# Per-head decays from running sums, with three small steps moved from VectorE to ScalarE, in a two-layer mLSTM/SSD trunk

## The reference

```python
acs = jnp.cumsum((dt * a_neg).reshape(bsz, nc, L, ng, ne), axis=2)
ah = jnp.transpose(acs, (0, 1, 3, 4, 2))
decay = jnp.exp(jnp.where(causal, ah[..., :, None] - ah[..., None, :], -jnp.inf))
y_intra = jnp.einsum('bcgts,bcgets,bcsgep->bctgep', cb, decay.astype(x.dtype), xw)
y_inter = (jnp.einsum('bctgn,bcgepn->bctgep', cc, s_start.astype(x.dtype))
           * jnp.exp(acs)[..., None].astype(x.dtype))
...
w_intra = jnp.exp(dlog - m_t[..., None])          # mLSTM: weights of the scores
ha = rmsnorm(ha, g_mlstm_head[i]).reshape(bsz, s_len, M_INNER) * jax.nn.sigmoid(o_pre)
```

## Time and profile before

| | |
|---|---|
| median of 3 runs | 1561.26 us (1561.2 to 1562.8) |
| profiled execution: its own time, its span | 1561.38 us, 1559.6 us |
| PE busy, share of the span | 1538.0 us, 99% |
| PEld busy | 1439.7 us, 92% |
| DVE busy | 1073.6 us, 69% |
| ACT busy | 809.2 us, 52% |
| POOL busy | 153.5 us, 10% |
| granted TensorE clock, mean | 0.999 of full |
| DMA | 271.09 MB, 174 GB/s mean |
| the mixing block's groups, layer 0 | 208 us to 453 us after the start |

### The profile page before, as it was taken

The page is one execution under the profiler, slowest core; times in us unless marked ns, Lnnn a source line. Parts: engine busy times, 40 slices in busy tenths (PEclk is TensorE's granted clock), DMA queues, the critical chain, the costliest instruction groups (busy, mean ns, idle before and its releaser), DMA issues.

```text
span 1559.6 us, 28133 instructions
## 1 busy us (share of the span) xinstructions
PE 1538.0 (99%) x11594; PEld 1439.7 (92%) x11594; DVE 1073.6 (69%) x1314; ACT 809.2 (52%) x1141; POOL 153.5 (10%) x147
## 2 busy tenths in 40 slices
PE   7999999999999999999999999999999999999998
PEld 6999999999999979999899999998999999799996
DVE  5556578889887546565765556799888866555556
ACT  6444385664655355443564445755766633544444
POOL 1000011233130000000000000113243100000001
PEclk9999999999999999999999999999999999999999
DMA  8665554456455556655565555454544465466551
GB/s 253 195 198 192 175 158 110 146 153 186 135 157 190 193 168 204 200 188 190 166 192 192 194 196 165 123 156 136 188 134 152 153 206 197 149 211 195 199 189 69
DMA packets 245089, 271.09 MB, mean 174 GB/s; under 512 B 12560, under 2 KB 226152, under 8 KB 245012
## 3 DMA queue, kind: packets, MB, share of 16 engines
q1 hardware_dynamic: 239504, 266.90, 53.6%
q10 hardware_dynamic: 5364, 2.98, 0.7%
q0 software_dynamic: 144, 0.15, 0.0%
HBM read 268.94 MB, written 1.05 MB: 173 GB/s over the span
## 4 chain that ended last, share of the span: by engine, by line
PE 90%; DVE 4%; issue 3%; ACT 2%; DMA 1%; SPq 0%; POOL 0%; ACTq 0%; POOLq 0%; DVEq 0%
PE bank L1562 29%; PE bank L1646 28%; PE bank L1592 8%; PE bank L1593 8%; PE bank L1594 8%; PE bank L1995 1%; PE bank L1587 1%; PE bank L1850 1%; DVE w_lo L936 1%; PE bank L1578 1%; PE bank L1580 1%; PE bank L1579 1%; ACT w_hi L530 1%; DVE xcv L1174 1%; DMA w_raw<-in_w_ffn_dram 1%
## 5 line engine op out<-in xcount | busy, mean ns | idle before, releaser
L936 DVE TENSOR_TENSOR w_lo<-w_raw,w_hi 128x2048 fp32r<-128x2048 f32 x248 | 576.9, 2328 | 315.8 <-ACT w_hi L530 315.5
L530 ACT ACTIVATE w_hi<-w_raw 128x2048 fp32r<-128x2048 f32 x248 | 474.1, 1916 | 307.4 <-PE bank L1646 131.0
L1646 PE MATMUL bank<-f_lo,w_hi 128*128 128x256 f32 x1280 | 355.6, 278 | 0.0
L1646 PE MATMUL bank<-f_hi,w_lo 128*128 128x256 f32 x1280 | 353.5, 276 | 0.0
L1646 PE MATMUL bank<-f_hi,w_hi 128*128 128x256 f32 x1240 | 342.6, 276 | 0.0
L1562 PE MATMUL bank<-u_hi,w_hi 128*128 128x256 f32 x1152 | 326.6, 283 | 1.3 <-DVE w_lo L936 1.3
L1562 PE MATMUL bank<-u_lo,w_hi 128*128 128x256 f32 x1152 | 319.9, 278 | 0.0
L1562 PE MATMUL bank<-u_hi,w_lo 128*128 128x256 f32 x1152 | 319.9, 278 | 0.0
L1646 PEld LDWEIGHTS bank<-f_hi,w_lo 128*128 128x128 f32 x1280 | 240.4, 188 | 0.0
L1646 PEld LDWEIGHTS bank<-f_lo,w_hi 128*128 128x128 f32 x1280 | 240.4, 188 | 0.0
L1646 PEld LDWEIGHTS bank<-f_hi,w_hi 128*128 128x128 f32 x1240 | 232.8, 188 | 0.0
(11 more groups left out here) (308 smaller groups left out, 2453.8 us busy)
## 6 DMA issues: line engine op xcount, KB each, us to landing
w_raw<-in_w_ffn_dram SPq DMA_DIRECT2D x262, 512.0 KB, 4.3
w_raw<-in_w_in_dram SPq DMA_DIRECT2D x160, 512.0 KB, 4.9
w_raw<-in_w_branch_b_dram SPq DMA_DIRECT2D x32, 512.0 KB, 4.4
w_raw<-in_w_branch_a_dram SPq DMA_DIRECT2D x16, 512.0 KB, 4.5
w_raw<-in_w_out_dram SPq DMA_DIRECT2D x16, 512.0 KB, 4.1
w_raw<-in_w_ple_gate_dram SPq DMA_DIRECT2D x16, 512.0 KB, 4.3
y_feat<-in_w_ple_dram ACTq DMA_DIRECT2D x2, 1024.0 KB, 4.9
h<-in_x_dram SPq DMA_DIRECT2D x2, 512.0 KB, 5.5
```

Of the source, the lines that this page charges most:

```text
L530: a_.activation(whi[slot][:, :, :], raw[slot][:, :, :], ACT.Copy).then_inc(sem["w_hi"], 1)
L936: v_.tensor_tensor(wlo[slot][:, :, :], raw[slot][:, :, :], whi[slot][:, :, :].bitcast(F32), ALU.subtract).then_inc(sem["w_lo"], 1)
L1646: i = mm(o, four(w[slot])[:, k, cs], x[:, rows0 + k, :], start=opens, stop=(not start and k == 3 and q == 2), skip_group_check=True)
```

## The change

Decays: a new matmul group in `gates(lay)`, once a layer, makes the running sums of all 32 heads as rows of `acs` (16 matmuls of 128 columns from `twin`, high and low part, with 40 stationary columns); ACT copies them out (`sums_high`), DVE subtracts the low part (`sums_low`). In each group PE then spreads a head's row over the partitions with `pick` (`sums(half)`: four matmuls of 256 columns, both chunks at once). ACT makes the distance by a Relu with the token's own sum as its bias (`acol`), one instruction for each head and chunk, then the exponentials. `R_hi`, `R_lo`, `segments` and `from_start` go. The scores' distances, the scaling of the normed heads and the output gate's last step go from DVE to ACT. DVE's order changes.

```diff
-                    def segments(c, half):
-
-                        pe.wait_ge(sem["r_built"], G * 4 + (2 * c + half + 1))
-                        mm(bank[4 + 2 * c + half][:, :], tri_gt_r[:, :], R_hi[half][:, :, :], start=True, stop=False)
-                        mm(bank[4 + 2 * c + half][:, :], tri_gt_r[:, :], R_lo[half][:, :, :], start=False, stop=True)\
-                            .then_inc(sem["seg_done"], 1)
-
-                    def from_start():
-                        for half in range(2):
-                            pe.wait_ge(sem["exp_done"], G * 4 + (3 + half))
-                            mm(bank[6 + half][:, :], ones_r[:, :], R_hi[half][:, :, :], start=True, stop=False)
-                            mm(bank[6 + half][:, :], ones_r[:, :], R_lo[half][:, :, :], start=False, stop=True)\
-                                .then_inc(sem["seg_done"], 1)
+                    def sums(half):
+
+                        if first:
+                            pe.wait_ge(sem["acs_ready"], lay + 1)
+                            pe.wait_ge(sem["pick_ready"], lay + 1)
+                            pe.wait_ge(sem["cum_exp"], lay + 1)
+                        elif half == 0:
+                            pe.wait_ge(sem["st_ready"], G)
+                            pe.wait_ge(sem["num1_ready"], G)
+                        else:
+                            pe.wait_ge(sem["y_ready"], G)
+                        for e in range(4):
+                            i = mm(bank[4 + 2 * half + e // 2][:, (e % 2) * S:(e % 2 + 1) * S], pick[half][:, e, :],
+                                   acs[:, bass.ds(g, 1), :].rearrange("p a b -> p (a b)"), start=True, stop=True)
+                        i.then_inc(sem["seg_done"], 1)
...
+                pe.wait_ge(sem["dA_split"], lay + 1)
+                for g in range(NG):
+                    for c in range(NC):
+                        o = bank[4 + g // 2][0:40, (g % 2) * S + c * P:(g % 2) * S + (c + 1) * P]
+                        mm(o, twin[0][:, c, g, :], tri_le_r[:, :], start=True, stop=False)
+                        i = mm(o, twin[1][:, c, g, :], tri_le_r[:, :], start=False, stop=True)
+                i.then_inc(sem["acs_done"], 1)
...
+                    def decay(half):
+
+                        act.wait_ge(sem["seg_done"], G * 2 + (half + 1))
+                        for e in range(4 * half, 4 * half + 4):
+                            for c in range(NC):
+                                i = a_.activation(seg[:, c, e, :], bank[4 + e // 2][:, (e % 2) * S + c * P:(e % 2) * S + (c + 1) * P],
+                                                  ACT.Relu, scale=-1.0, bias=acol[:, c, bass.ds(g * EH + e, 1)])
+                        i.then_inc(sem["gap_ready"], 1)
+                        for e in range(4 * half, 4 * half + 4, 2):
+                            a_.activation(cs[:, e:e + 2, :], two(4 + e // 2)[:, :, P:2 * P], ACT.Exp)
+                        act.wait_ge(sem["gap_ready"], G * 2 + (half + 1))
+                        a_.activation(seg[:, :, 4 * half:4 * half + 4, :], seg[:, :, 4 * half:4 * half + 4, :],
+                                      ACT.Exp, scale=-1.0).then_inc(sem["exp_done"], 1)
 
                     def score_exp():
+                        act.wait_ge(sem["gtk_ready"], G + 1)
+                        act.wait_ge(sem["scores_done"], G + 1)
+                        for c in range(NC):
+                            i = a_.activation(pm[:, c, :], bank[3][:, S + c * P:S + (c + 1) * P], ACT.Relu, bias=gtk[:, c:c + 1])
+                        i.then_inc(sem["d_ready"], 1)
                         act.wait_ge(sem["d_ready"], G + 1)
                         a_.activation(pm[:, :, :], pm[:, :, :], ACT.Exp, scale=-1.0).then_inc(sem["p_exp"], 1)
...
+                    def heads_normed():
+                        act.wait_ge(sem["hsc_ready"], G + 1)
+                        for c in range(NC):
+                            i = a_.activation(num[:, c, 0:MV], num[:, c, 0:MV], ACT.Copy, scale=hsc[:, c:c + 1])
+                        i.then_inc(sem["hn_ready"], 1)
...
+                    act.wait_ge(sem["group_ready"], G + 1)
+                    act.wait_ge(sem["o_tanh"], G * 3 + 1)
+                    for t in range(2):
+                        a_.activation(osg[:, t, :], osg[:, t, :], ACT.Identity, scale=ghn[:, t:t + 1], bias=ghn[:, t:t + 1])\
+                            .then_inc(sem["o_tanh"], 1)
...
                     else:
                         dve.wait_ge(sem["taps_ready"], G + 1)
                         evac(BC, xin[:, 0, :, 3:])
+                        step(1)
+                        queries_and_keys()
                         taken(BC)
                         conv(0, 0, (0, 1), bcv[:, :, :])
-                        queries_and_keys()
-                        step(1)
+                        step(2)
                         silu(0, bcv[:, :, :])
-                        step(2)
-                        distances()
                         step(3)
...
                         conv(2, 0, (4, 5), xcv[:, 2:4, :])
+                        mask_cb()
                         silu(2, xcv[:, 2:4, :])
-                        mask_cb()
                         step(4)
                         dve.wait_ge(sem["ysum_ready"], G + 1)
                         evac(Z0, zs[:, 0:2, :])
+                        weighted_inputs()
                         step(5)
-                        weighted_inputs()
                         gate_half(0)
```

More of the change, by code:

```diff
@@ L112, in trunk @@
         top[0] = place(feat_at, 512, 1024)
+        ha_hi_at = top[0]
         ha_hi = sb("ha_hi", [P, 2 * MH, S], F32R)
+        ha_lo_at = top[0]
         ha_lo = sb("ha_lo", [P, 2 * MH, S], F32R)
+        last_group = 2 * (MH - 1) * S * 4
+        pick = [at(f"pick{b}", [P, EH // 2, P], F32R, off + last_group)[0] for b, off in enumerate((ha_hi_at, ha_lo_at))]
         top[0] = place(top[0], 512, 1024)
@@ L186, in trunk @@
         late = a
-        xwe_at = late + NC * EH * HP * 4
+        twin = [at(f"twin{b}", [P, NC, NG, 40], F32R, late + b * 40 * NC * NG * 4)[0] for b in range(2)]
         xw, a = at("xw", [P, NC, EH * HP], F32, a)
@@ L643, in body, with sums_high @@
                     G = act.snap(lay * NG + g)
[L645 to L654, removed]
+                    def sums_high():
+                        act.wait_ge(sem["acs_done"], lay + 1)
+                        for b in range(2):
+                            i = a_.activation(acs[0:40, 2 * b:2 * b + 2, :],
+                                              bank[4 + b][0:40, :].rearrange("p (g s) -> p g s", g=2), ACT.Copy)
+                        i.then_inc(sem["acs_hi"], 1)
                     def step(p):
@@ L673, in tanh_conv @@
                         a_.activation(cth[:, :, :], dst, ACT.Tanh).then_inc(sem["tanh_done"], 1)
[L675 to L682, removed]
@@ L796, in body @@
                     step(8)
+                    if not first:
+                        heads_normed()
                     scaled(O)
                     a_.activation(osg[:, :, :], osg[:, :, :], ACT.Tanh, scale=0.5).then_inc(sem["o_tanh"], 1)
+                    act.wait_ge(sem["group_ready"], G + 1)
[3 more added lines that the diff above has]
+                            .then_inc(sem["o_tanh"], 1)
                     if first:
                         step(9)
-                    if not last:
-                        act.wait_ge(sem["yi_done"], G + 1)
-                        act.wait_ge(sem["zth_ready"], G * 2 + 2)
-                        for half in range(2):
-                            part_of(R_hi, dA_hi, g + 1, 0, half)
-                        act.wait_ge(sem["y_done"], G + 1)
-                        for half in range(2):
-                            part_of(R_lo, dA_lo, g + 1, 0, half).then_inc(sem["r_built"], 1)
                     act.wait_ge(sem["ha32_ready"], G + 1)
@@ L1194, in split_heads @@
                         return x.rearrange("p (e d) -> p e d", e=EH)
-                    def distances():
-                        dve.wait_ge(sem["gtk_ready"], G + 1)
-                        dve.wait_ge(sem["scores_done"], G + 1)
-                        for c in range(NC):
-                            i = v_.tensor_scalar(pm[:, c, :], bank[3][:, S + c * P:S + (c + 1) * P], gtk[:, c:c + 1],
-                                                 0.0, ALU.subtract, ALU.max)
-                        i.then_inc(sem["d_ready"], 1)
                     def mask_cb():
@@ L1370, in body @@
                                             op0=ALU.mult, op1=ALU.mult).then_inc(sem["y_ready"], 1)
-                    dve.wait_ge(sem["o_tanh"], G + 1)
-                    for t in range(2):
-                        ch.add(v_.tensor_scalar(osg[:, t, :], osg[:, t, :], 1.0, ghn[:, t:t + 1], ALU.add, ALU.mult))
-                    ch.wait()
+                    dve.wait_ge(sem["o_tanh"], G * 3 + 3)
                     dve.wait_ge(sem["hnT_done"], G + 1)
@@ L1880, in body @@
```

(13 more changed lines are left out.)

109 lines of the change are left out of this document (58 added, 51 removed).

## The result

The changed kernel takes 1585.04 us (median of 4 runs, 1584.63 to 1585.31) against 1561.47 us: a ratio of 1.0149, 95% interval 1.0134 to 1.0164. It is slower by 23.6 us, where +10.1 us was forecast. The profiled execution has its own time at 1585.14 us.

A forecast was written before the change was run, and what follows sets the result against it. PE, 99% busy, was taken to bound the kernel if DVE, ACT and POOL deliver in time. Groups of +0.4, +3.05, +0.8, +0.8 make 5.05 us a layer, 10.1 for two: 1571.4 us (chance 0.48), range 1552 to 1577.

The forecast's parts named there:

- PE's own work: Looped group on PE: segments and from_start go (2.8 us), sums come (0.94 us), so 1.85 us shorter.
- The port: Looped groups: early cbm lets POOL's product hold up silu and w_lo; Z1 7.9 us after cbm, PE waits 2.65 us.
- Rivals 1 and 2: At Z1: 1, silu wins the port, 1560.1 us, chance 0.17; 2, w_lo is not held up, 1552.6 us, chance 0.18.
- Rival 3: Whole kernel: the whole gain arrives, in the first groups too, 1545 us; chance 0.07.
- Rival 4: First group on ACT: a Relu with bias costs 0.1 us more than the copies, 1575 us; chance 0.10.
- The first group: Each layer's first group: ACT's longer chain delays tanh and O; second group starts about 268.4 against 268.02, +0.4 us.
- The step that failed: Looped group after Z1's start: the rest of the loop taken as 39.8 less 0.93, 38.85 us.
- the looped group: Third and fourth groups: period 62.1 us against 61.3, 0.8 us slower each.
- The second group: Second group of a layer: Z1 starts at 313.8, before at 309.70; +3.05 us besides the first group's 0.4.
- one layer: Sum over a layer's four groups: 0.4 + 3.05 + 0.8 + 0.8 = 5.05 us slower.
- TensorE's own saving: PE's work in the groups of one layer: 6.3 us less if nothing came late.

The follow-up runs named there:

- the run with the first group's old tail: Changed kernel with DVE's old order in each first group's tail (first half of gate, Z1 scaling, heads' scales, last unit's w_lo): 1580.17 us, 1.0109.
- The filled run: Changed kernel plus 20 unread 256-column matmuls on PE ahead of Z1's wait for its weights in each looped group: 1575.23 us, 1.0081.

## Why the prediction was half right

**PE's own work** was forecast at -1.85 us a loop and is -1.59: `from_start` gives 0.91 (0.93 forecast), the sums give 0.68 in place of 0.92. The forecast took 0.47 us for a pair of `segments`, from its start to the next matmul's. But the 48 matmuls between the pairs, in pieces of 12 and 36, took 5.46 us; in one piece they take 5.66 us in the changed kernel and 5.65 us elsewhere in the loop of the kernel before. So a pair set PE back by 0.40 us only.

**The port** came as written: POOL first by 0.2 us, silu 2.76, `w_lo` 4.44, Z1 8.03 us after `cbm` (7.9), 23.55 us after the scores (23.25), the wait 2.71 us (2.65). Moved alone it makes the kernel before slower by the same amount, and holding POOL back undoes it. Rivals 1 and 2 needed a silu or a `w_lo` that isn't held up, and are out. Rival 3, the whole gain, is out too. Rival 4 needed Relus that cost 0.1 us more than the copies; eight of them take 2.17 us, where eight copies took 2.18, and DVE waits 3.71 us for the tanh, not 5. ACT, then DVE, first group:

```profile
237.00 2.17 ACT L687 ACTIVATE seg<-bank,acol 128x128 f32<-128x128 f32 x8
```

```profile
247.55 0.69 DVE L1215 SCALAR_TENSOR_TENSOR xcv<-cth,xcv 128x512 f32<-128x512 f32 x1 [3.71 <-ACT cth L680]
```

**The first group** was forecast at +0.4. The second group's first matmul is at 268.52 in place of 268.02, and PE waits 0.87 us at O (about 1 forecast).

**The step that failed** is the one that reads "The rest of the loop is 39.8 less 0.93 = 38.85". From Z1 to the next scores it takes 40.82 us. It was taken over from a trace in which PE never stands still for as long as 1 us in the mixing blocks, and the clock is at its upper level throughout them; the price of an idle stretch was set at its length. Of the 1.97 us missing, 1.74 is Z1 itself at the lower clock and 0.23 the sums. So the looped group, at +0.8, measures +3.09. The second group, at +3.05, measures +5.0: Z1 starts 0.7 us later than forecast, since `cbm` is 0.6 us later, and Z1 then takes 6.96 us where it took 5.55. The lateness that this group takes over from the first was in the forecast, with 2.0 us at DVE's first evacuation; the run with the first group's old tail gives 1.8 us of it back. In layer 0:

| counted at the sums on PE | forecast | measured |
|---|---|---|
| first group | +0.4 | +0.5 |
| second group | +3.05 | +5.0 |
| third group | +0.8 | +3.1 |
| fourth group | +0.8 | +3.1 |
| one layer | +5.05 | +11.7 |

The filled run gives the clock's part for the whole kernel: 9.8 of the 13.6 us by which the forecast was short. No rival had it, so the range ended at 1577 us. Of the other 3.8 us, 0.7 us lie in each second group (Z1 later than forecast) and 0.5 us in each later one (0.3 at Z1, 0.2 in the sums).

That the loss is an order and not the new arithmetic shows in the best version: the same sums, Relus and copies, with three pieces of order changed and one wait on POOL, take 1553.98 us, 0.5% less than before and 31 us less than the changed kernel. TensorE's own saving was forecast at 6.3 us a layer if nothing came late. Of it 4.3 us arrive: from the first scores to the end of the groups in layer 0 it is 226.9 us, where the kernel before takes 231.3.

## What to carry to other kernels

When an instruction that releases POOL is moved ahead, ask which DVE instructions with two SBUF operands come next: if one of them is on the critical path, hold POOL back with a wait, and keep the early release for the engines that don't share the port. Price a wait of TensorE of some 2 us or more at its length plus the slow matmuls that may follow it: here 1.4 to 1.7 us where the clock fell at Z1, 2.6 to 2.8 us where it stayed low for longer (the second groups of the run with the first group's old tail), and nothing in the 10 cases of 31 in which it didn't fall. And before a gain is booked to an edit, see in which pieces of the kernel it lies and whether the granted clock changed there.

## What the runs showed of the hardware

A wait costs more than its length, and not always the same. Over the changed kernel and the twelve experiments, the granted clock fell to 0.50 (1.2 GHz) behind 6 of 6 waits of 3.3 us, 6 of 8 of 2.7 us, and 9 of 17 between 1.96 and 2.21 us; behind none that stood alone at 1.6 us or less. In each of these cases PE had not waited as long as 1 us at a stretch in the 20 us before. The first 20 us of the program, where PE waits several times, are left out. The same wait could go either way: the changed kernel's 1.99 us at X01 of the second group is followed by 0.50 in layer 0 and by 1.00 in layer 1. What decides it in one case and not in the other stays open. The Trainium skill, page "TensorE: Matmul & The Clock Gate", section "What's actually happening", has the lower level as the resting state that activity lifts; these rows agree, with some 3 us at half clock after most falls and some 6 us in the second groups of the run with the first group's old tail (313.4 to 319.4).
